# Starting two chunks of an output projection between attention units, in PSUM banks that were score banks

## What is computed

```python
def hybrid_mixing(h, w_in, ..., w_out, pos):
    z = h @ w_in
    ya = mla_mixer(...)     # 6 heads, causal attention in blocks of 128 queries
    yb = pool_mixer(...)    # windowed means, width 256
    yc = fox_mixer(...)     # 6 heads, causal attention with a decay
    return jnp.concatenate([ya, yb, yc], axis=-1) @ w_out

def second_block(x, ...):
    for l in range(DEPTH):                      # DEPTH = 2
        x = x + 0.5 * swiglu(rmsnorm_2(x, ffn1_norm[l]), ...)
        x = x + hybrid_mixing(rmsnorm_2(x, mix_norm[l]), ...)
        x = x + 0.5 * swiglu(rmsnorm_2(x, ffn2_norm[l]), ...)
    return rmsnorm_2(x, final_norm)
```

## Time and profile before

| | |
|---|---|
| median of 3 runs | 3454.08 us |
| lowest, highest | 3450.94, 3455.11 us |
| span of the profiled execution | 3452.0 us |
| PE busy, weight loads busy | 3368.6 us (98%), 2783.9 us (81%) |
| DVE, ACT, POOL busy | 1837.6, 1202.7, 389.1 us |
| granted TensorE clock, mean | 0.990 |
| the two attention stages of block 2, from unit 30 on | from 2049.9 us and from 3001.1 us |

### The profile page before, as it was taken

One profiled execution on the slowest core, in us unless ns is written; L12 is line 12 of the kernel. 1 busy time (PEld: TensorE's weight loads), 2 busy tenths in 40 slices (PEclk: granted clock), 3 DMA queues, 4 the chain that ended last, 5 costly groups with the idle time before them and its releaser, 6 DMA issues.

```text
span 3452.0 us, 47261 instructions
## 1 busy us (share of the span) xinstructions
PE 3368.6 (98%) x17188; PEld 2783.9 (81%) x17188; DVE 1837.6 (53%) x2786; ACT 1202.7 (35%) x1886; POOL 389.1 (11%) x416
## 2 busy tenths in 40 slices
PE   7999999999999999999999999999999999999998
PEld 5878888888877788888888677888888886778887
DVE  6777866455358444454345665434543456654343
ACT  4464312122157322333232473323332324633232
POOL 0023100000202200020001242000200011420001
PEclk8999999999999999999999999999999999999999
DMA  6301333343220233333333312333333333123332
GB/s 233 114 27 60 103 108 121 122 133 110 67 68 19 61 98 94 96 91 101 95 96 107 82 32 74 102 93 95 91 100 97 94 101 79 32 74 97 93 97 92
DMA packets 551252, 314.76 MB, mean 91 GB/s; under 512 B 31102, under 2 KB 524888, under 8 KB 551128
## 3 DMA queue, kind: packets, MB, share of 16 engines
q1 hardware_dynamic: 550608, 312.99, 30.4%
q10 hardware_dynamic: 520, 0.13, 0.0%
HBM read 310.98 MB, written 2.10 MB: 91 GB/s over the span
## 4 chain that ended last, share of the span: by engine, by line
PE 89%; DVE 5%; ACT 3%; issue 1%; DMA 1%; POOL 1%; SPq 0%; DVEq 0%; ACTq 0%; POOLq 0%
PE ps L900 26%; PE ps L902 25%; PE ps L904 25%; PE ps L1498 2%; PE ps L1464 2%; DVE scr L2196 1%; PE ps L1429 1%; PE ps L995 1%; PE ps L996 1%; PE ps L994 1%; DVE nmax L2475 1%; ACT w_hi_sb L1534 1%; PE ps L1033 1%; DMA scr<-in_w_mod 1%; DVE hl_lat L2184 1%
## 5 line engine op out<-in xcount | busy, mean ns | idle before, releaser
L1959 DVE TENSOR_TENSOR w_lo_sb<-w_raw,w_hi_sb 128x1024 fp32r<-128x1024 f32 (+1 forms) x460 | 588.9, 1280 | 1157.8 <-ACT w_hi_sb L1534 1156.2
L1534 ACT ACTIVATE w_hi_sb<-w_raw 128x1024 fp32r<-128x1024 f32 (+1 forms) x460 | 506.5, 1101 | 1306.5 <-PE ps L904 1276.9
L900 PE MATMUL ps<-hh_lat,w_lo_sb 128*128 128x512 f32 x1712 | 680.0, 397 | 11.8 <-DVE z L2064 6.1
L902 PE MATMUL ps<-hl_lat,w_hi_sb 128*128 128x512 f32 x1712 | 668.7, 391 | 0.0
L904 PE MATMUL ps<-hh_lat,w_hi_sb 128*128 128x512 f32 x1712 | 668.4, 390 | 0.0
L900 PEld LDWEIGHTS ps<-hh_lat,w_lo_sb 128*128 128x128 f32 x1712 | 322.0, 188 | 84.5 <-issue 11.4
L902 PEld LDWEIGHTS ps<-hl_lat,w_hi_sb 128*128 128x128 f32 x1712 | 322.3, 188 | 68.0 <-issue 4.3
L904 PEld LDWEIGHTS ps<-hh_lat,w_hi_sb 128*128 128x128 f32 x1712 | 321.8, 188 | 66.6
L900 PE MATMUL ps<-h2h,w_lo_sb 128*128 128x512 f32 x704 | 275.2, 391 | 1.9 <-DVE z L2435 1.5
L900 PE MATMUL ps<-m2h,w_lo_sb 128*128 128x512 f32 x704 | 273.9, 389 | 0.0
L902 PE MATMUL ps<-h2l,w_hi_sb 128*128 128x512 f32 x704 | 273.9, 389 | 0.0
(11 more groups left out here) (389 smaller groups left out, 5495.6 us busy)
## 6 DMA issues: line engine op xcount, KB each, us to landing
w_raw<-in_ffn_w_gu SPq DMA_DIRECT2D x176, 512.0 KB, 3.8
w_raw<-in_w_ff SPq DMA_DIRECT2D x128, 512.0 KB, 4.0
w_raw<-in_ffn_w_down SPq DMA_DIRECT2D x64, 704.0 KB, 4.5
z<-in_w_mod SPq DMA_DIRECT2D x64, 512.0 KB, 5.1
w_raw<-in_w_in SPq DMA_DIRECT2D x56, 512.0 KB, 3.8
w_raw<-in_w_out SPq DMA_DIRECT2D x32, 512.0 KB, 3.8
scr<-in_w_mod SPq DMA_DIRECT2D x16, 512.0 KB, 5.1
scr<-in_w_mod SPq DMA_DIRECT2D x2, 2048.0 KB, 15.3
```

The costliest lines, as they stand in the source:

```text
L900: mm = nc.tensor.matmul(dst, wl, hi[:, k, 0:n], start=(k == 0), stop=False)
L902: mm = nc.tensor.matmul(dst, wh, lo[:, k, 0:n], start=False, stop=False)
L1534: nc.scalar.activation(w_hi_sb[:, slot, 0:width], w_raw[:, slot, 0:width], ACT.Copy).then_inc(S["w_hi"], 1)
L1959: nc.vector.tensor_tensor(w_lo_sb[:, slot, 0:width], w_raw[:, slot, 0:width], w_hi_sb[:, slot, 0:width].bitcast(F32), ALU.subtract).then_i ...
```

## The change

PE begins chunks 0 and 1 of the output projection between the units 35 to 46, in banks 0 and 1: five tiles of each (3, 4, 0, 1, 2), 30 matmuls, two or three to a unit. After the last unit it makes tiles 5 and 6 of chunk 0, of chunk 1, then tile 7 of chunk 0 and of chunk 1. The scores stay in banks 2 and 3 to the end, and `scores(u)` waits for the exponential of unit u-2 throughout. DVE adds chunks 0 and 1 from banks 0 and 1; its first pair is written out instead of being a turn of the loop. ACT, POOL and SP have the same instructions in the same order.

```diff
-                b = 2 + u % 2 if u < S_WIDE else u % 4
+                b = 2 + u % 2
             return ps[:, b * BANK:b * BANK + n]
-
-        def s_depth(st, u):
-
-            return 2 if st.first or u < S_WIDE else 4
...
+        OUT_FROM, OUT_TO = 35, 47
+        OUT_EARLY, OUT_LATE = (3, 4, 0, 1, 2), (5, 6, 7)
...
+                def early_out(st, u):
+
+                    r, n = st.out, 3 * len(OUT_EARLY)
+                    steps_of = OUT_TO - OUT_FROM
+                    for i in range(2 * n * (u - OUT_FROM) // steps_of, 2 * n * (u - OUT_FROM + 1) // steps_of):
+                        c, (k, j) = i // n, divmod(i % n, 3)
+                        k = OUT_EARLY[k]
+                        if i % n == 0:
+                            pe.wait_ge(S["w_lo"], r.chunk0 + c + 1)
+                            pe.wait_ge(S["z_taken"], st.z2.at("z_taken", len(Z2_TILES)))
+                            pe.wait_ge(S["pool_lo"], st.mixer.at("pool_lo", 2))
+                        if c == 0 and j == 0 and k < 3:
+                            pe.wait_ge(S["ao_lo"], st.at("ao_lo", k + 1))
...
+                        if st.block2 and st.group is None:
+                            for late in (OUT_LATE[:-1], OUT_LATE[-1:]):
+                                for c in range(2):
+                                    for k in late:
...
+                                    if k == OUT_LATE[-1]:
+                                        mm.then_inc(S["chunk_done"], 1)
+                            run_mixed(st, taken)
...
-                            if st.at("p_exp", u + 1 - s_depth(st, u)) > 0:
-
-                                pe.wait_ge(S["p_exp"], st.at("p_exp", u + 1 - s_depth(st, u)))
-                            if not st.first and u in (S_WIDE, S_WIDE + 1):
-                                pe.wait_ge(S["z_taken"], st.z2.at("z_taken", len(Z2_TILES)))
+                            if st.at("p_exp", u - 1) > 0:
+
+                                pe.wait_ge(S["p_exp"], st.at("p_exp", u - 1))
...
                                 scores(u)
                                 if not st.first:
                                     beside_units(st, u)
+                                if not st.first and OUT_FROM <= u < OUT_TO:
+                                    early_out(st, u)
...
-                        def pair(c, nkt):
+                        def pair(c, nkt, first_bank=2):
...
-                                        x, bank({"lat": 2, "ctx": 6}[name] + s, W[name]), st.gate(name, c + s), x,
+                                        x, bank({"lat": first_bank, "ctx": 6}[name] + s, W[name]), st.gate(name, c + s), x,
...
-                        if feeds(st):
+                        if st.spec.get("attention"):
+                            pair(0, st.kt, 0)
+                            with dve.Fori(1, 3) as i:
+                                pair(i * 2, st.kt)
+                            pair(6, next_kt(st))
+                        elif feeds(st):
```

More of the change, by code:

```diff
@@ L322, in build_program @@
                           gate=one, group=None, final=True, kt=KD, prep=(R_F2 + KD * l, h2h, h2l), block2=True, attention=att)
+                    att.spec["out"] = stages[-1]
                 else:
@@ L1088, in beside_units @@
                                          start=True, stop=True).then_inc(S["chunk_done"], 1)
+                def early_out(st, u):
[10 more added lines that the diff above has]
+                            pe.wait_ge(S["ao_lo"], st.at("ao_lo", k + 1))
+                        wh = w_hi_sb[:, c, k * P:(k + 1) * P]
+                        wl = w_lo_sb[:, c, k * P:(k + 1) * P]
+                        hi, lo = mixed_tile(r, k)
+                        if j == 0:
+                            nc.tensor.matmul(bank(c), wl, hi, start=(i % n == 0), stop=False)
+                        elif j == 1:
+                            nc.tensor.matmul(bank(c), wh, lo, start=False, stop=False)
+                        else:
+                            nc.tensor.matmul(bank(c), wh, hi, start=False, stop=False)
                 def turn_y(st, tiles, rows):
@@ L1353, in taken @@
                             pe.wait_ge(S["r_taken"], c + (st.at("r_taken", 0) + s - 1))
[L1354 to L1359, removed]
+                        if st.block2 and st.group is None:
+                            for late in (OUT_LATE[:-1], OUT_LATE[-1:]):
+                                for c in range(2):
+                                    for k in late:
+                                        if c == 0:
+                                            pe.wait_ge(S["ao_lo"], st.at("ao_lo", k - 7))
+                                        wh = w_hi_sb[:, c, k * P:(k + 1) * P]
+                                        wl = w_lo_sb[:, c, k * P:(k + 1) * P]
+                                        hi, lo = mixed_tile(st, k)
+                                        nc.tensor.matmul(bank(c), wl, hi, start=False, stop=False)
+                                        nc.tensor.matmul(bank(c), wh, lo, start=False, stop=False)
+                                        mm = nc.tensor.matmul(bank(c), wh, hi, start=False, stop=(k == OUT_LATE[-1]))
+                                    if k == OUT_LATE[-1]:
+                                        mm.then_inc(S["chunk_done"], 1)
+                            run_mixed(st, taken)
+                        elif st.group is None:
+                            pe.wait_ge(S["gm_lo"], st.at("gm_lo", 0))
+                            order = (4, 5, 6, 7, 0, 1, 2, 3)
                             for c in range(2):
@@ L1363, in _ @@
                                 for k in order:
-                                    if c == 0 and k in ao:
-                                        pe.wait_ge(S["ao_lo"], st.at("ao_lo", ao.index(k) + 1 - len(ao)))
+                                    if c == 0 and k < 4:
+                                        pe.wait_ge(S["ao_lo"], st.at("ao_lo", k - 3))
                                     dst = bank(down_banks["lat"] + c)
@@ L1368, in _ @@
                                     wl = w_lo_sb[:, c, k * P:(k + 1) * P]
[L1369 to L1372, removed]
+                                    nc.tensor.matmul(dst, wl, hh_lat[:, k, :], start=(k == order[0]), stop=False)
+                                    nc.tensor.matmul(dst, wh, hl_lat[:, k, :], start=False, stop=False)
+                                    mm = nc.tensor.matmul(dst, wh, hh_lat[:, k, :], start=False, stop=(k == order[7]))
                                 if "ctx" in st.sets:
@@ L1375, in _ @@
                                 mm.then_inc(S["chunk_done"], 1)
[L1376 to L1379, removed]
+                            run_linear(st, taken, down_banks, h, splits=[(2, st.chunks, st.sets)])
                         elif tail(st):
```

## The result

The changed kernel takes **3468.43 us** (median of 5 runs, 3467.57 to 3471.12) against 3454.08 before: +14.35 us, a ratio of 1.0039 with a 95% interval of 1.0028 to 1.0049.

The account below looks back on a forecast made before the run. PE, busy 98% of the span, was taken to bound the kernel; per layer +2.1 - 1.3 + 0.65 + 2.65 = +4.1 us, in both +8.2 on the median of 3454.08, gave 3462.3 us, range 3456 to 3469.

Parts of the forecast that it names:

- The front: Units 32 to 36: scores wait for exponentials, the first moved matmul for DVE's pool tiles; 2.1 us lost a layer.
- The rest of the units: From unit 36 on, moved matmuls cover PE's pauses and the shallower score ring costs nothing; 1.3 us gained a layer.
- the moved matmuls' cost: In the attention stage, the first moved matmul behind scores takes 0.28 us instead of 0.227; 0.65 us lost a layer.
- Behind the stage: Chunks 0 and 1 end 0.68 us apart, so PE waits before chunk 2 for DVE's adding; 2.65 us lost a layer.
- The sum: Per layer +2.1 - 1.3 + 0.65 + 2.65 = +4.1 us, in both +8.2, giving a median of 3462.3 us; chance 0.46.
- The clock: New pauses at units 33 to 35 and behind chunk 1 may halve PE's clock; a fall costs 1.6 us.
- this rival: Clock falls at the new pauses: two more give 3465.5 us, all four 3468.7; chance 0.22.
- the bounds of the structure: Limits of the summed terms without the clock: +0.95 to +5.5 us a layer, 3456 to 3465 us.
- the pause of 3.03 us: Among the first attention units of both layers in the trace before; the clock fell after the second layer's only.
- The Trainium skill's rule: A matmul engine pausing between bursts begins the next at half clock, so each new pause costs something each time.
- The free front: Pool tiles ready before 2059.3, late scores hidden, the front costs nothing: +2.0 us a layer, 3458.1 us; chance 0.28.
- A gain: All PE's pauses go and chunk 2's weights come without a pause: -2.35 us a layer, 3449.4 us; chance 0.04.

Follow-up runs that it names:

- front_only: The kernel before, with two score banks instead of four in units 32 to 47 of block 2 and nothing moved: 3458.13 us, ratio 1.0005.
- fill_front: The changed kernel with 14 idle matmuls in the three waits before unit 33's scores, unit 35's scores and the first moved matmul: 3465.3 us, ratio 1.0025.
- heads_first: The changed kernel with the moved tiles in order 0, 1, 2, 3, 4, so the pool tiles are needed three tiles later: 3463.73 us, ratio 1.0023.
- fill_back: The changed kernel with ten idle matmuls in the wait before chunk 2, in both layers of block 2: 3465.43 us, ratio 1.0028.
- back_only: The kernel before, with only chunks 0 and 1 reordered to end as in the changed kernel, nothing moved, four score banks: 3462.24 us, ratio 1.0017.

## Why the prediction was right, and where it was not

- **The front, 2.1 us lost: right.** Behind the zero, in us: unit 33's scores 4.47 (forecast 4.4, from 2055.3), the first moved matmul 9.79 (9.78, from 2060.65), and, at full clock, the transposes of unit 31 10.32 (10.28) and unit 36's scores 11.66. Without the two moved matmuls (0.54) these last stand at 11.12, in the kernel before at 9.01: 2.1 us. The pool tiles are where they were, so DVE was not late. The idle time shown before the first moved matmul was 1.20 us in the second layer (forecast 1.3) and 0.76 in the first, where half clock had stretched the work ahead of it.
- **The rest of the units, 1.3 gained less 0.65 for the moved matmuls' cost: right, and 0.4 too careful.** At full clock the attention part costs 38.59 - 30.69 - 6.81 = 1.09 us in place of 1.45. No transposes wait from unit 36 to 43. That the ring is covered by PE's own work holds: front_only, without that work, waits at units 40 and 41.
- **Behind the stage, 2.65 lost: right.** The excess is (6.80 - 18 x 0.227) less what the kernel before had over 48 x 0.227, 2.6 us. DVE's adding ends the wait, not the weights, and neither tile 7 nor chunk 3 waits. Left out was the restart: the first matmuls behind a wait are further apart, which costs 0.14 us (32.55 against 32.41).
- **The sum, +4.1 a layer: 3.86 measured** with both waits filled; +8.2 for the kernel was +7.7 in that trace and +8.2 in its medians.
- **The clock: the wrong step.** Its price was right (1.6 us forecast, 1.59 measured). The forecast gave the falls only a chance of 0.22 and made none of them the likeliest; all four came, in both traces of the kernel. That the measured time still lies in the range is owed to the upper end, which was set at this rival; the bounds of the structure ended at 3465. 3462.3 + 4 x 1.59 = 3468.7, the end of that rival, against 3468.4 measured. The error lies in the working, not in a missing row. The trace had shown the pause of 3.03 us with a fall in one layer of two, which is even chances for each new place, as far as that trace tells. With four places that makes two falls likeliest and none a matter of one in sixteen, if they are independent. "Not fixed by the program" was read as a reason to leave the cost out, where it was a reason to count half of it. That alone gives 3465.5. Even chances were themselves a rough reading: in the 14 traces of this document the pause of 3.03 us has a fall at it in ten of the 14 second layers and in none of the first.
- **The Trainium skill's rule** (TensorE: Matmul & The Clock Gate, "HAM oscillation — how this bites in real kernels"), that an engine that pauses between bursts begins the next one cold, gives 3468.7 when it is applied to each new pause, as the prediction quotes it. But that section speaks of pauses that are long enough, and its example waits longer than any new wait here, so with its condition it names no fall and 3462.3. The changed kernel had all four falls, but over all traces the runs bear out neither reading. Of the twelve places in these traces with the wait of 2.42 us, eight have a fall behind them.
- **The free front** (3458.1) is out: its point of decision, DVE's pool tiles 1.2 us earlier, did not come. A gain did not come from this change, but it was to be had from the same idea.

Open: what decides whether the clock falls behind the same pause. Two traces of one kernel agree in all four places, but the same rows in both layers of fill_front have a fall in one, and in heads_first neither pause behind the stage has one. PE's own work since the zero does not decide it either. The changed kernel (two traces), fill_back, heads_first and front_only have the same PE rows, with the same wait of 1.36 us, from the zero until a clock falls or to unit 35. Yet in six of the eight layers of the first four traces the clock falls 4.3 to 6.6 us behind the zero, and in front_only in neither layer. No run here varied the moment of the pause alone.

## What to carry to other kernels

Before you move work forward to fill pauses, look at what it covered where it stood: these 24 matmuls of chunk 1 were the cover under which ACT and DVE prepared chunk 2. Moving one chunk instead of two, and keeping a bank more for the scores, turned +14 us into -3 (by the traces; -2.6 by the medians). Give each new wait of an engine with a throttled clock two prices, the wait and the fall behind it, and where the trace shows a fall at one of two like waits, count a share of it for each (here 8 of 12 places behind the stage); filling the wait with idle matmuls gives the second price back. Where totals scatter by as much as the effect, compare the two traces over the stretch that the change touches.

## What the runs showed of the hardware

- A fall of the granted clock to 0.50 cost 1.59 us, behind the wait of 2.42 us as in front. In the second layer of the changed kernel it came after three shorter waits (1.36, 0.63 and 1.20 us) with work between; in its first layer, and in both layers of fill_back and heads_first, after or at the end of the first of them alone; in back_only once behind a single pause of 1.07 us. In front_only the waits of 1.36 and 0.63 us brought none.
- Idle matmuls in the wait kept the clock at 1.00 in every place where they stood, eight of eight (unfilled, the wait behind the stage had a fall in 8 of 12 places and the front of the narrower ring with moved matmuls in 8 of 8), and delayed the matmul behind them by 0.04 us at most.
- Behind the wait before chunk 2, filled or not and with the clock at 1.00, the second matmul starts 0.34 us after the first and the rows are dense (0.227 us) again two matmuls on: 0.14 us for each restart.
